# Layer 0's first modulation weights: one-row products on TensorE between the in-projection's blocks, in place of VectorE's weighted sums

## The reference, cut to what matters

```python
cond = jax.nn.silu(c)                                # c: (1, 1024)
for i in range(DEPTH):                               # DEPTH = 2
    mod = cond @ ada_w[i] + ada_b[i]                 # ada_w[i]: (1024, 6144)
    sh1, sc1, g1, sh2, sc2, g2 = jnp.split(mod[:, None, :], 6, axis=-1)
    h = rms_norm(x, norm1_g[i]) * (1.0 + sc1) + sh1
    y = diff_attention(h, ...)                       # layer 0: q, k, v = split(h @ w_in, 3); w_in: (1024, 3072)
    x = x + g1 * y
    h = rms_norm(x, norm2_g[i]) * (1.0 + sc2) + sh2
    y = hierarchical_moe(h, ...)                     # 32 experts
    x = x + g2 * y
```

## Time and profile before

| | |
|---|---|
| time, median of 3 runs (lowest, highest) | 1850.01 us (1849.89, 1850.33) |
| the profiled execution's own time | 1846.84 us |
| its span, from the first to the last instruction | 1845.0 us |
| mean granted TensorE clock | 0.972 |
| PE busy in the span | 1684.1 us (91%) |
| DVE busy | 490.1 us (27%) |
| ACT busy | 444.2 us (24%) |
| POOL busy | 158.4 us (9%) |
| moved by DMA | 585.12 MB, mean 317 GB/s |

### The profile page before, as it was taken

How to read it: one execution, slowest core, us unless ns; L and a number is a source line. 1 busy time by engine, 2 the same in 40 slices (tenths; PEclk the granted TensorE clock), 3 DMA queues, 4 the chain that set the end, 5 groups by cost and what they waited for, 6 DMA issues and landing times.

```text
span 1845.0 us, 18530 instructions
## 1 busy us (share of the span) xinstructions
PE 1684.1 (91%) x7537; PEld 859.2 (47%) x7537; DVE 490.1 (27%) x935; ACT 444.2 (24%) x939; POOL 158.4 (9%) x236
## 2 busy tenths in 40 slices
PE   6896999888889879999999999999998999989988
PEld 4643543333333334845464344444443356565564
DVE  1357221000000103244241002221220123553362
ACT  2015211111111102015231013333331034343351
POOL 0212010000000010123000010000001000100000
PEclk9999999999999999999989999999998999999999
DMA  9989779999999999987369989999999963413310
GB/s 359 347 337 397 296 277 409 422 419 420 422 421 421 421 413 396 383 338 258 115 244 410 347 323 397 395 405 420 420 419 410 368 231 107 145 50 117 137 46 23
DMA packets 122752, 585.12 MB, mean 317 GB/s; under 512 B 11936, under 2 KB 16872, under 8 KB 99008
## 3 DMA queue, kind: packets, MB, share of 16 engines
q1 hardware_dynamic: 101008, 489.59, 66.3%
q0 software_dynamic: 21536, 88.72, 13.1%
q10 hardware_dynamic: 112, 5.51, 0.8%
HBM read 578.87 MB, written 21.32 MB: 325 GB/s over the span
## 4 chain that ended last, share of the span: by engine, by line
PE 60%; DMA 25%; DVE 6%; ACT 3%; issue 3%; SPq 3%; ACTq 0%; DVEq 0%; POOL 0%
PE psum L2204 57%; DMA ring<-in_expert_w_up 19%; DMA work<-in_ada_w 3%; SPq L1433 1%; PE psum L699 1%; DMA ring<-in_expert_w_gate 1%; SPq L1402 1%; DMA work<-in_ctx 1%; DMA ring<-in_ada_w 1%; DMA work<-in_w_mod 1%; PE psum L2508 1%; DVE small L1057 1%; PE psum L1198 1%; DVE work L1882 1%; DVE work L2099 0%
## 5 line engine op out<-in xcount | busy, mean ns | idle before, releaser
L2204 PE MATMUL psum<-ring,work 128*64 128x512 f32 (+5 forms) x4272 | 1095.4, 575 | 66.8 <-DMA ring<-in_expert_w_up 53.9
L2204 PEld LDWEIGHTS psum<-ring,work 128*64 128x64 f32 (+2 forms) x4272 | 424.3, 152 | 664.5 <-issue 635.0
L2204 PE MATMUL psum<-work 128*128 128x192 f32 (+9 forms) x1048 | 218.2, 371 | 8.1 <-DVE work L2032 2.6
L2204 PEld LDWEIGHTS psum<-work 128*128 128x128 f32 (+3 forms) x1048 | 144.9, 188 | 105.2 <-issue 81.6
L2099 DVE TENSOR_TENSOR work<-work,psum 128x256 f32<-128x256 f32 x64 | 27.0, 421 | 593.2 <-ACT work L1802 593.2
L1802 ACT ACTIVATE work<-psum 128x256 f32<-128x256 f32 x64 | 24.5, 383 | 607.7 <-PE psum L2204 607.7
L2204 PE MATMUL psum<-work,ring 128*128 128x256 f32 x704 | 158.8, 384 | 3.2 <-DMA ring<-in_diff_w_in 1.1
L2204 PEld LDWEIGHTS psum<-work,ring 128*128 128x128 f32 x704 | 133.4, 192 | 29.1 <-issue 8.1
L1669 ACT ACTIVATE work<-psum 128x256 f32<-128x256 f32 (+5 forms) x184 | 79.7, 443 | 224.7 <-PE psum L2508 76.0
L1561 POOL DMA_INDIRECT expert_rows<-work,targets x56 | 55.1, 984 | 806.6 <-DVE work L2125 806.6
L2125 DVE TENSOR_TENSOR work<-psum,rows 128x512 f32<-128x512 f32 x64 | 44.3, 692 | 255.8 <-PE psum L2204 255.7
(11 more groups left out here) (295 smaller groups left out, 956.6 us busy)
## 6 DMA issues: line engine op xcount, KB each, us to landing
ring<-in_expert_w_gate SPq DMA_DIRECT2D x60, 2048.0 KB, 16.5
ring<-in_expert_w_up SPq DMA_DIRECT2D x60, 2048.0 KB, 17.4
ring<-in_expert_w_down SPq DMA_DIRECT2D x57, 2048.0 KB, 14.4
work<-in_ada_w POOLq DMA_DIRECT2D x40, 1024.0 KB, 8.0
ring<-in_w_in SPq DMA_DIRECT2D x12, 2048.0 KB, 10.1
work<-in_w_mod POOLq DMA_DIRECT2D x16, 1024.0 KB, 6.8
ring<-in_sb_w_in SPq DMA_DIRECT2D x6, 2048.0 KB, 24.7
ring<-in_w_out SPq DMA_DIRECT2D x6, 2048.0 KB, 8.0
```

What stands on the lines that cost most here:

```text
L2204: return T.matmul(out_, lhsT, rhs, start=start, stop=stop, skip_group_check=True)
```

## The change

`SUMMED` loses groups 1 and 2, so that the items 0 to 15 are multiplied on PE like those of group 3. DVE's 16 passes over them are gone; `ada_take` of both groups stays. PE does two items behind each of the blocks 2 to 10 of the in-projection, 18 in all: the 16 and the first two of group 3. The six others of group 3 stay in the attention, behind the steps 2 to 7, and the steps 8 and 9 have none. All else, with the semaphores' counts, stays; the waits that `ada_used` ends are now ended by PE's items in place of DVE's passes.

```diff
-    SUMMED = (1, 2, 5, 6)
+    SUMMED = (5, 6)
...
-            for g in SUMMED[2 * l:2 * l + 2]:
-                ada_sum(g)
+            for g in (1, 2) if l == 0 else SUMMED:
+                if g in SUMMED:
+                    ada_sum(g)
                 ada_take(g)
...
             if g in SUMMED:
                 pe.wait_ge(sem("ada_sum"), SUMMED.index(g) + 1)
-                pe.wait_ge(*((sem("ada_row"), g - 1) if g > 1 else (sem("first_line"), 3)))
+                pe.wait_ge(sem("ada_row"), g - 1)
...
             pe.wait_ge(sem(f"ada_in{i % 3}"), in_count(i))
             if t == 0:
-                pe.wait_ge(sem("ada_row"), g - 1)
+                pe.wait_ge(*((sem("ada_row"), g - 1) if g > 1 else (sem("first_line"), 3)))
...
-        QKV_ITEMS = [[[KT * SUMMED[2 * l + (i == 11)] - 1] if i in (6, 11) else [] for i in range(12)] for l in range(2)]
-        DIFF_ITEMS = share_out(16, [0, 0] + 8 * [1] + [0, 0] + 4 * [1, 0])
+        QKV_ITEMS = [share_out(0, [0, 0] + 9 * [2] + [0]), [[KT * SUMMED[i == 11] - 1] if i in (6, 11) else [] for i in range(12)]]
+        DIFF_ITEMS = share_out(18, [0, 0] + 6 * [1] + 4 * [0] + 4 * [1, 0])
```

## The result

The changed kernel took 1859.11 us (median of 8 runs, 1853.29 to 1862.04), the kernel before 1847.78 us in the 8 runs beside it (1845.48 to 1850.33). The ratio is 1.0058 with a 95% interval of 1.0045 to 1.0071, or 8.3 to 13.1 us, 10.7 in the middle: slower, as forecast, in the forecast range of 1852.8 to 1861.5, and on the dear side of the forecast's +7.0. The profiled execution took 1861.62 us with a span of 1859.8, 14.8 more than the span before. Single runs of one kernel scatter by 5 to 9 us, and this one is the second longest of its 8; so a profile says where time lies, and the timed ratio how much it is.

What follows compares the result with a forecast made beforehand. In-projection bound by PE's matmuls plus one stall, attention mostly by DVE's rhythm; 17.5 added less 11.9 removed, plus 3.7 late items, less 2.25 in attention terms, gives +7.0 us, 1857.0; own range +4 to +10, 8 in 10 from 1852.8 to 1861.5.

Steps and rivals of the forecast that it cites:

- Added on PE: In-projection: 18 items of four matmuls at 0.97 us each, all on PE's path, 17.5 us.
- Removed: PE's path to block 11's end: wait behind block 6, item 7, block 7's slow clock and a small gap go, 11.9 us.
- Late items: In-projection: PE stalls for late loads of item 3 (1.3 us) and item 5 (2.4), +3.7 us, bounds 0 and 6.3.
- rival 2: In-projection: late items also halve PE's clock, up to 3.0 us more for one stall, +10.0 in all; chance 0.2.
- Blocks of 7 us on both sides keep PE busy: In-projection: the argument given against a slow clock behind the stalls; no size of its own.
- Into the attention: From block 11 to the first scores: 2.83 us in place of 3.46, a gain of 0.6 us.
- In the attention: Attention: waits for late items go, 1.35 us, and one short wait of DVE for PE, 0.3 us.
- Downstream: After the attention: the out-projection and expert stage move with PE, so the shift is passed on in full.
- The sum: Whole kernel: 5.6 + 3.7 - 0.6 - 1.35 - 0.3 = +7.0 us, or 1857.0 us.
- Rival 1: In-projection: no item is late, DMA keeps up and PE runs through; +3.3 us, 1853.3; chance 0.2.
- rival 4: In-projection: no effect, PE's items overlap the blocks' matmuls to a good part; +0.3 us; chance 0.05.
- rival 3: Attention: faster, since fewer items and none late shorten every step from 2 to 15; chance 0.05.

Runs made afterwards that it cites:

- e3: Changed kernel with each of the 18 in-projection items multiplied twice, the extra products into an unused bank; ratio 1.0117 to the kernel before.
- e9: Kernel before with nine small loads (lambda vectors, layer 0's router weights) issued by SP behind the last in-projection slice instead of POOL; ratio 0.9974.
- e1: Changed kernel with the router's four small loads issued behind item 13 in place of item 4; ratio 1.0048 to the kernel before.
- e8: Changed kernel again without an edit, for a second profile; one run, span 1858.0 us.
- e11: Changed kernel with the nine small loads issued by SP behind the last in-projection slice instead of POOL; ratio 1.0043 to the kernel before.
- e7: Kernel before again without an edit; ratio 1.0006, span 1845.4 us.
- e2: Changed kernel with sixteen items in the in-projection, group 3's first two put back into the attention; ratio 1.0069 to the kernel before.
- e4: Kernel before with item 7 added up behind block 7 in place of block 6; ratio 0.9991.
- e10: Kernel before with the nine small loads on SP and item 7 behind block 7 in place of block 6; ratio 0.9984.
- e5: Kernel before with group 1 still summed on DVE, item 7 behind block 7, and group 2 multiplied on PE, mostly in the attention; ratio 1.0091.

## Why the prediction was right

**Added on PE: 17.5 us forecast.** Nine pairs at 1.83 us are 16.5, and e3 gives 0.84 to 0.86 for one more item. The forecast's 0.97 of item 15 was at a granted clock of 1.00, from 129.76 to 130.73. Each block between items takes up to 0.1 us more than in the long stretch of 28.09 us in the earlier trace rows (7.06 to 7.11 from start to next start, for 7.02), 0.7 in all. The term holds.

**Removed: 11.9 us.** The wait of 7.15, item 7 (1.82 to the next start), block 7 at half clock (granted 0.50 from 92 to 96 us, and 9.30 us long) and the 0.77 are all gone from the timeline after. With 16.5 + 4.4 + 2.9 - 11.9 = 11.9 and 1.2 in longer blocks, longer pairs and gaps, the 13.1 at the end of block 11 is accounted for. What this term did not say is how weak the wait was: by e9 it hung on nine small loads in POOL's order.

**Late items: 1.3 + 2.4 = 3.7 us, bounds 0 and 6.3.** Measured 0.34 + 4.04 = 4.4, at the two items named and at no other. Item 3 took 5.7 us from issue to use, between the 5.2 and 7.9 of before. For item 5 the working has a slip: 64.7 + 12.2 is 76.9 and not 76.2, so that its stall should have read 3.1 and not 2.4, the term 4.4, and the sum +7.7. The measured 4.4 fits that. From item 3's use to item 5's it took 13.15 us (64.05 to 77.20) for the 12.2 forecast and the 15.2 of before; from issue to use item 5 took 12.3 us, like the 12.5 of before, and that number alone would have given 3.6. e1 shows the cause: without the router's loads in between, the wait is 0.34.

**The clock: this is the step that was mis-sized.** I had given it 0.2 as rival 2, at +3.0 us for a wait of 2.4, and left it out of the sum. Both profiles of the changed kernel have it: 0.85 + 2.05 = 2.9 us behind the 4.04, 1.6 in the block behind the 3.92 of e8; e11 has 1.7 in the block behind a wait of 2.41. e1, with waits of 0.34, has none. The granted clock in these blocks, from the windows of PE (length, busy, clock, DMA share, GB/s) of the changed kernel and then of e11, is 0.50:

```profile
78.00:80.00 2.00, 2.00 (x10) 0.50 1.04 433
80.00:82.00 2.00, 2.00 (x6) 0.50 0.99 388
```

```profile
114.00:116.00 2.00, 2.00 (x3) 0.50 0.94 386
```

"Blocks of 7 us on both sides keep PE busy" was the wrong half of the argument. Full blocks of 7 us stood around all six such waits in the in-projection, from 7.15 and 5.67 us (before, e7) over 4.08, 4.04 and 3.92 (e2, the changed kernel, e8) down to 2.41 (e11), and the block behind each took 1.6 to 2.2 us longer.

**Into the attention: 0.6 us.** 2.84 us behind block 11 for a forecast 2.83.

**In the attention: -1.65 us, and this gain did not come.** From first scores to the down load it took 97.00 and 96.30 us before, 99.25 and 98.25 after: 1.3 to 3 longer. The other runs narrow that. With before's items in the attention e4, e9 and e10 took 98.72, 98.17 and 98.05, with the changed kernel's e1, e3 and e11 took 98.22, 97.50 and 97.50. The means of five profiles each are 97.65 and 98.14: no gain, and a loss no larger than the scatter. The waits of the earlier trace rows are gone. The windows of PE from 150 us (length, busy, clock, DMA share, GB/s), of before and then of the changed kernel, show what came in their place:

```profile
150.00:175.00 25.00, 16.60 (x110) 0.92 1.01 413
175.00:200.00 25.00, 22.22 (x84) 0.94 1.06 424
```

```profile
150.00:175.00 25.00, 19.71 (x116) 0.77 0.94 368
175.00:200.00 25.00, 18.80 (x94) 0.72 0.93 385
```

The granted clock is 0.77 and 0.72 for 0.92 and 0.94 (0.88 and 0.99 in e7, 0.77 and 0.82 in e8). These windows don't hold the same steps in both kernels. Those from 25 to 50 us behind the first scores do better, of before and then of the changed kernel:

```profile
157.91:182.91 25.00, 16.00 (x95) 0.86 1.01 419
```

```profile
170.40:195.40 25.00, 18.64 (x92) 0.70 1.01 422
```

In the same stretch it is 0.86, 0.91, 0.80 and 0.80 in e7, e4, e9 and e10, and 0.71, 0.70, 0.72 and 0.73 in e8, e1, e3 and e11. So the lower clock comes with the change, but what it costs is not shown. Whether it is the four steps without an item, in which PE does less, was not tried by itself; e2, which has items behind two of them, has 0.59 there, and late items.

**Downstream: passed on in full.** 14.74 us at the down load, 14.8 in the span; the layer 0 expert stage moves as a block. The first expert load, for which I had 158.5, goes out at 162.95, mostly since the scores themselves begin 12.5 us late and not 8.7. In single profiles layer 1 adds or takes 3 us by chance (e7, e1). Over the nine timed experiments with an edit, the shift at the down load and the timed difference agree within 2.4 us (e3 21.4 and 21.6, e5 15.3 and 16.8); only for the changed kernel itself are they 4 apart, 14.7 and 10.7, which is not explained beyond the scatter of a mark.

**The sum.** +7.0 us forecast, +10.7 measured by the ratio (8.3 to 13.1), +13.0 and +14.8 by the spans of the two profiles against the first of before. The mechanism of the in-projection was right, with the price of one wait's clock left out and the attention's gain not there. It is rival 2, at +10.0, that happened: +10.7 lies outside the forecast's own +4 to +10, and 1859.11 is inside the range by the room that rival 2 had been given. The kernel before was also 2.2 us faster in these 8 runs than in the three that I started from, which brought the absolute time closer to the forecast than the difference is. Rival 1 (+3.3) is ruled out by item 5's wait and by the interval, rival 4 (+0.3) by e3, rival 3, faster, by the interval.

## What to carry to other kernels

A wait that looks like a slow engine may be a late transfer: ahead of moving sums from VectorE to a TensorE that has no gaps, look at what sits between the items in the queue that loads them. Here nine small loads put elsewhere were worth 4.8 us, and 18 products on the busy engine, which took the same wait away, cost 10.7 net. Work fed through a few buffers is best consumed at a steady rate: in e5 DMA moved 72 GB/s from 100 to 125 us, for 353 before, while POOL's next load waited 20.82 us for a buffer (to 113.15), and the items postponed to a stage with room on the engine found no room in DMA, 12 waits and 25.1 us. And where TensorE waits for a DMA between full blocks, a slow block behind it belongs in the price; here all four such waits of 2.41 to 4.08 us in the in-projection (e11, e8, the changed kernel, e2) had one.

## What the runs showed of the hardware

- Four one-column products of 512 columns at four output strips take 0.84 to 0.86 us on PE's path between blocks (e3, granted clock 1.00 from 110 to 150 us), while eight 128x512 products with full columns take 7.13. At 7.13 / 8 = 0.89 us each, four would take 3.6 one behind another: they run side by side. They don't run beside the blocks: with 18 items more, block 11 ended 15.1 us later (e3 against e1).
- The granted clock fell after shorter waits than I had thought: a wait of 2.41 us between blocks (e11) left the next block of 7.13 us at 8.83, with 0.50 from 114 to 116 us; one of 3.92 (e8) left 8.77, with 0.66 from 80 to 82, and one of 4.04 left 9.22 for 7.17, with 0.50 from 80 to 82. Waits of 0.34 to 0.68 us left none. In the attention the same wait of 2.19 us was followed by an item in 1.82 us in the first profile of before (0.50) and in 1.08 in e7 (1.00 from 132.1 to 133.2), so a short wait does not always bring it.
- A 1 MB load took 12.3 us from issue to use with the router's four small loads, 162 KB, issued ahead of it, and 9.5 us without them (e1, 64.06 to 73.52); the five lambda loads, and item 4 behind them, stood ahead of it in both.
